# Two steps' attention scores issued together into the two halves of a PSUM bank

## What is computed

```python
h = rms_norm(x, g_mix);  proj = h @ w_in            # q, k, v of both kinds, two gates
ya = moba_attention(qa, ka, va, bias_a)             # 8 heads, causal
yb = swa_attention(qb, kb, vb, sinks, bias_b)       # 8 heads, window 128, a sink each
merged = sigmoid(ga + ...) * (ya @ w_branch_a) + sigmoid(gb + ...) * (yb @ w_branch_b)
x = x + merged @ w_out
x = x + square(relu(rms_norm(x) @ w_ff1)) @ w_ff2
```

## Time and profile before

| what | value |
|---|---|
| median of 3 runs | 724.69 us (723.51 to 725.76) |
| profiled execution | 726.15 us, its span 724.4 us |
| mean granted TensorE clock | 0.995 |
| PE busy | 709.8 us, 98% |
| PEld (weight loads) busy | 580.1 us, 80% |
| DVE, ACT, POOL busy | 382.3, 312.3, 331.8 us |
| attention stage (steps 0 to 31) | from 125.8 to about 277 us of the span |
| DMA | 96 GB/s in the mean |

### The profile page before, as it was taken

The page is one execution under the profiler, slowest core; times in us unless marked ns, Lnnn a source line. Parts: engine busy times, 40 slices in busy tenths (PEclk is TensorE's granted clock), DMA queues, the critical chain, the costliest instruction groups (busy, mean ns, idle before and its releaser), DMA issues.

```text
span 724.4 us, 9461 instructions
## 1 busy us (share of the span) xinstructions
PE 709.8 (98%) x3434; PEld 580.1 (80%) x3434; DVE 382.3 (53%) x551; ACT 312.3 (43%) x572; POOL 331.8 (46%) x207
## 2 busy tenths in 40 slices
PE   8898999999999999899999999999999999999998
PEld 6686888888888888787888888888888888888887
DVE  5786653455445453886875521255113551166787
ACT  7575773566656554553443411333212431233220
POOL 4464664455554444343344454344444344344442
PEclk9999999999999999999999999999999999999999
DMA  8221333222221211442322322322322322322231
GB/s 272 85 88 59 111 102 111 75 73 75 86 80 54 88 58 59 138 142 99 108 96 90 114 87 93 111 87 87 116 87 87 110 93 87 115 88 88 89 115 58
DMA packets 22910, 69.89 MB, mean 96 GB/s; under 512 B 2731, under 2 KB 4267, under 8 KB 22876
## 3 DMA queue, kind: packets, MB, share of 16 engines
q1 hardware_dynamic: 22876, 69.44, 29.1%
HBM read 67.27 MB, written 2.16 MB: 96 GB/s over the span
## 4 chain that ended last, share of the span: by engine, by line
PE 88%; DVE 7%; ACT 1%; DMA 1%; issue 1%; SPq 1%; DVEq 0%; ACTq 0%
PE bank L882 27%; PE bank L883 26%; PE bank L884 26%; PE bank L996 3%; PE bank L1007 2%; DVE probs L800 2%; PE bank L1024 2%; PE bank L1026 1%; DVE store L617 1%; DMA w_raw<-slabs 1%; DVE probs L790 1%; DVE x_lo L802 1%; DVE probs L788 1%; DVE store L621 1%; ACT x_hi L542 1%
## 5 line engine op out<-in xcount | busy, mean ns | idle before, releaser
L308 POOL TENSOR_TENSOR w_lo<-w_raw,w_hi 128x1024 fp32r<-128x1024 f32 x111 | 268.3, 2417 | 295.8 <-ACT w_hi L369 295.8
L882 PE MATMUL bank<-x_hi,w_hi 128*128 128x512 f32 (+1 forms) x600 | 237.5, 396 | 3.4 <-DVE x_lo L608 2.1
L883 PE MATMUL bank<-x_lo,w_hi 128*128 128x512 f32 (+1 forms) x600 | 232.6, 388 | 0.0
L884 PE MATMUL bank<-x_hi,w_lo 128*128 128x512 f32 (+1 forms) x600 | 232.5, 387 | 0.0
L369 ACT ACTIVATE w_hi<-w_raw 128x1024 fp32r<-128x1024 f32 x112 | 118.5, 1058 | 142.2 <-PE bank L884 142.2
L882 PEld LDWEIGHTS bank<-x_hi,w_hi 128*128 128x128 f32 x600 | 113.0, 188 | 34.9 <-issue 5.1
L884 PEld LDWEIGHTS bank<-x_hi,w_lo 128*128 128x128 f32 x600 | 113.0, 188 | 23.6
L883 PEld LDWEIGHTS bank<-x_lo,w_hi 128*128 128x128 f32 x600 | 113.1, 188 | 21.4
L882 PE MATMUL bank<-qk_hi,w_hi 128*128 128x512 f32 x320 | 125.9, 394 | 1.8 <-DVE w_lo L796 1.8
L884 PE MATMUL bank<-qk_hi,w_lo 128*128 128x512 f32 x320 | 125.3, 391 | 0.0
L883 PE MATMUL bank<-qk_lo,w_hi 128*128 128x512 f32 x320 | 125.1, 391 | 0.0
(11 more groups left out here) (103 smaller groups left out, 649.4 us busy)
## 6 DMA issues: line engine op xcount, KB each, us to landing
w_raw<-slabs SPq DMA_DIRECT2D x112, 512.0 KB, 3.3
store<-x_t SPq DMA_DIRECT2D x16, 256.0 KB, 2.8
bias_m<-tab_dram SPq DMA_DIRECT2D x8, 256.0 KB, 4.5
out<-store SPq DMA_DIRECT2D x7, 256.0 KB, 2.0
bias_m<-tab_dram SPq DMA_DIRECT2D x8, 128.0 KB, 3.8
w_raw<-slabs SPq DMA_DIRECT2D x2, 384.0 KB, 5.7
w_raw<-slabs SPq DMA_DIRECT2D x2, 128.0 KB, 4.4
out<-store SPq DMA_DIRECT2D x2, 128.0 KB, 1.7
```

The costliest lines, as they stand in the source:

```text
L308: pool.tensor_tensor(w_lo[:, g % WS, :], w_raw[:, g % RAW, :], w_hi[:, g % WS, :].bitcast(F32), ALU.subtract).then_inc(w_lo_ready, 1)
L882: pe.matmul(out_, wh, xh, start=first, stop=False)
L883: pe.matmul(out_, wh, xl, start=False, stop=False)
L884: last = pe.matmul(out_, wl, xh, start=False, stop=end)
```

## The change

Where two steps' scores fit one bank side by side, `scores` issues both steps' passes at the even step, the second step's into columns 256 and up of the same bank, and nothing at the odd one. This is so for steps 0 to 15 in pairs (256 and 256 columns, or 256 and 128) and for the last two steps of each causal pair (256 and 128 columns: steps 18 and 19, 22 and 23, 26 and 27, 30 and 31). The causal steps with 512 and 384 columns stay single. The wait for `max_ready` stays at every step that issues scores, and is gone from the 12 odd steps that issue none. `scores_max` of an even step of a pair waits for two units more, that is for the second step's scores in the same bank. Transposes, gate halves and values stay where they were; the number of matmuls is the same.

```diff
+        def scores_at(i, e, qt):
+            at = S // 2 if (qt % 2 == 0 if i < 8 else qt == 0) else 0
+            return bank[3 + e][:, at:at + P * key_tiles(i, qt)[1]]
+
+        def score_steps(step):
+            if STEPS // 2 <= step and step % QT < 2:
+                return (step,)
+            return (step, step + 1) if step % 2 == 0 else ()
...
             def scores_max(u, i, e, qt):
...
-                dve.wait_ge(scores_done, u + 1)
+                step = u // 2
+                dve.wait_ge(scores_done, u + 3 if len(score_steps(step)) == 2 else u + 1)
...
-                    out=probs[:, u % 4, 0:n], in0=bank[3 + e][:, 0:n], in1=bias_m[:, i % 4, 0:n],
+                    out=probs[:, u % 4, 0:n], in0=scores_at(i, e, qt), in1=bias_m[:, i % 4, 0:n],
...
             def scores(step):
-                if step:
+                steps = score_steps(step)
+                if step and steps:
                     pe.wait_ge(max_ready, 2 * step)
-                for a in range(3):
-                    for u, i, e, qt in units(step):
+                for of in steps:
+                    for a in range(3):
+                        for u, i, e, qt in units(of):
...
-                        last = pe.matmul(bank[3 + e][:, 0:P * nk], q, k, start=(a == 0), stop=(a == 2))
+                            last = pe.matmul(scores_at(i, e, qt), q, k, start=(a == 0), stop=(a == 2))
```

More of the change, by code:

```diff
@@ L987, in scores @@
             def scores(step):
-                if step:
+                steps = score_steps(step)
+                if step and steps:
                     pe.wait_ge(max_ready, 2 * step)
-                for a in range(3):
-                    for u, i, e, qt in units(step):
-                        k0, nk = key_tiles(i, qt)
-                        q = (qk_lo if a == 1 else qk_hi)[HEADS[e], q_tile(i), P * qt:P * qt + P]
-                        k = (qk_lo if a == 2 else qk_hi)[HEADS[e], k_tile(i), P * k0:P * (k0 + nk)]
-                        last = pe.matmul(bank[3 + e][:, 0:P * nk], q, k, start=(a == 0), stop=(a == 2))
-                        if a == 2:
-                            last.then_inc(scores_done, 1)
+                for of in steps:
+                    for a in range(3):
+                        for u, i, e, qt in units(of):
+                            k0, nk = key_tiles(i, qt)
+                            q = (qk_lo if a == 1 else qk_hi)[HEADS[e], q_tile(i), P * qt:P * qt + P]
+                            k = (qk_lo if a == 2 else qk_hi)[HEADS[e], k_tile(i), P * k0:P * (k0 + nk)]
+                            last = pe.matmul(scores_at(i, e, qt), q, k, start=(a == 0), stop=(a == 2))
+                            if a == 2:
+                                last.then_inc(scores_done, 1)
             def probs_transpose(step):
```

## The result

The changed kernel takes 718.72 us (median of 7, 717.36 to 722.05); the kernel before took 725.06 us in the same sessions (median of 7, 723.51 to 726.65). The ratio is 0.9913, with a 95% interval of 0.9893 to 0.9934. The profiled execution took 718.83 us, its span 717.0 us against 724.4.

A forecast was written before the change was run, and what follows sets the result against it. PE's own stream was taken to bound the attention stage. Merges giving 1.5, 1.4 and 2.4 us, together 5.3 us, came off the 724.69 us median, forecasting 719.4 us, range 717.4 to 722.1 us.

The forecast's parts named there:

- What bounds the stage: Attention stage: bound by PE's own stream, so time taken out of it comes off unless a wait replaces it.
- The hole is the array's change of mode, not the wait: Ahead of scores on PE: 0.17 us hole in all 32 steps, from changing 128-row columns to 64-row halves, not `max_ready`.
- The odd steps: Twelve odd steps lose their scores group: 0.68 us removed with 128 columns, 0.74 us with 256.
- The added passes: Even step's group on PE: three further passes add 0.36 us with 256 columns, 0.34 us with 128.
- dear seam: Rival: second step's passes start afresh, each merge pays 0.55 us; gain 2.8 us, 721.9 us; chance 0.10.
- DVE's wait: Even step's `scores_max` waits for both steps' scores: sliding chain moves 0.34 to 0.36 us, causal chain 0.08 us.
- The stall itself: PE's wait for `y_sums` before `values` at steps 18, 22, 26, 30: 0.40 us, falling to 0.14 us.
- The small waits inside `values`: PE's 0.15 us wait at steps 6, 10 and 14 neither grows nor goes.
- The sum: Twelve merges: 1.5 us and 1.4 us from sliding pairs, 2.4 us from causal ones, together 5.3 us.
- a case by itself: Clock rival: fall to 1.2 GHz behind the attention absent (717.8 us) or twice as long (721.0 us); chance 0.10.

The follow-up runs named there:

- the kernel before with `y_sums` first: Kernel before the change, with DVE's `y_sums` put ahead of `gate_scale` in steps 6, 10, ... 30; median 722.52 us, ratio 0.9966.
- the two kernels without it: Kernel before and changed kernel, each with DVE's `y_sums` ahead of `gate_scale`; medians 722.52 and 717.82 us, steps 18 and 19 together 10.80 and 10.45 us.
- the run with the waits: Changed kernel with the 12 waits for `max_ready` put back at the odd steps that issue no scores; median 719.92 us, ratio 0.9934.
- that with `y_sums` first: DVE's `y_sums` put ahead of `gate_scale`, nothing else; run on the changed kernel (717.82 us) and on the kernel before (722.52 us).
- the kernel with split groups: Changed kernel with the second step's scores moved behind the first three gate matmuls of the even step, without a wait; median 730.86 us, ratio 1.0103.
- the one with the sliding half alone: Changed kernel with pairs of steps for the sliding heads only, every causal step issuing its own scores; median 721.22 us, ratio 0.9963.

## Why the prediction was right

- **What bounds the stage.** PE's own stream: what was taken out of it came off the time, and nothing behind the attention gave it back (5.69 us at the end of the loop and at the end of the stall alike).
- **The hole is the array's change of mode, not the wait.** That it comes with the group is shown from both sides: 12 waits with no group cost 0.17 us in all, 12 groups with no wait 0.43 us each where nothing else waits. That within the group it is the change from 128 rows to two halves of 64, and the array running empty for it, is argued: from the loads that start only with their matmuls, and from the ends that grow with the matmul in front. The Trainium skill, TensorEngine Tiling (Array Packing), section Key Properties, says that changing the tiling mode drains TensorE. The runs agree with it for the halves of the rows.
- **The odd steps.** Forecast 0.68 and 0.74 us, and the rows 0.69 us from transposes to the second gate product as forecast. By whole steps the odd ones are 0.67 to 0.71 us shorter with 128 columns and 0.75 to 0.78 with 256.
- **The added passes.** Forecast 0.34 us for three of 128 columns, measured 0.29: the one behind the seam's first needed 0.06 us and not 0.11. The dear seam fell.
- **DVE's wait.** Its start 0.31 us behind the last pass held exactly. At the causal steps the chain moved by 0.04 us and not 0.08, as the passes cost 0.29 and not 0.34 us, and the hole ahead of `values` fell to 0.17 us at step 18 (0.18 forecast) and 0.21 at the other three. The causal merges were worth 0.65 us each (0.60 forecast). The stall itself was sized too large, at 0.40 us: that is the hole in the weight loads, while PE lost 0.30 to 0.32 us by it, as the kernel before with `y_sums` first shows. It did not spoil the sum, because that goes by DVE's chain, which sets the length of the step in both kernels. The small waits inside `values` at steps 6, 10 and 14 were to stay at 0.15 us and grew to 0.21: DVE's second `y_sums` moved by 0.29 us, and PE reached `values` only 0.24 us later, as its 12 gate products took 2.85 us and not 2.89. Why they did is open. That it is the stall that takes up the difference is shown by the two kernels without it, 0.35 us.
- **The sum.** Forecast 5.3 us. The attention gave 5.7 (5.30 in the stretch and 0.4 for the first merge, ahead of it): the forecast was 0.4 us short. Most of it is some 0.05 us at each of the eight merges with a 128-column step (on PE in the sliding ones, in DVE's chain in the causal ones), the rest 0.02 to 0.03 us at each of the others.
- **The rest of the median.** The medians stand 6.3 us apart in the first session, and 6.7 (725.04 and 718.34) in the one in which the changed kernel was run again. With a mean clock of 0.997 and more on both sides they stand 4.9 apart. So the difference of the medians can't be told from 5.7 more closely than by about 1 us either way; in the two profiles the clock's part is 1.6 us, and seen. That the measured 718.72 us lies so near the forecast 719.4 is partly luck: a fall of the clock more or less moves an execution by more than that distance. The prediction had this as a case by itself, and set it against one fall behind the stall only; falls also come and go at 8 and at 26 us.

## What to carry to other kernels

Where matmuls that use half the array's rows stand between full ones, count the groups and not the matmuls: here a group cost 0.4 us in its ends and 0.1 us for each further pass. Putting two groups together is worth that, as long as the reader of the shared bank has time to wait for both. Before pricing such a merge, look whether PE stands idle a little later in the same step: a longer group in front of an idle hole was nearly free (0.04 us), and a merge was worth 0.65 us there where it gave 0.35 without the hole. And size such a hole by the matmuls, or by a run without it: in the weight loads it looked larger (0.44 us) than what it cost (0.30 to 0.32).

## What the runs showed that was not expected

- A wait on a semaphore whose value is long there costs PE nothing that shows: 12 of them made 0.17 us, no more than the 0.23 us between two profiles of one kernel.
- The second pass of 128 columns starts 0.06 us behind the first where the three follow the seam, and 0.16 us behind it at the head of a group of its own; the third follows the second by 0.11 us in both the earlier trace rows.
- Matmuls on half of the array's columns stand among full ones without a hole, 0.17 us for a pair of the two kinds; those on half of its rows don't.
- The granted clock falls to the 1.2 GHz level in some executions and not in others of the same kernel, in three places: at 8 us, at 26 us and behind the stall near 290 us. A fall lasts for over 3 us, at 26 us in the run with the waits and at 8 us in that with `y_sums` first for over 6. In the profiles of the kernel with split groups and of the one with the sliding half alone none of them is there, in the others one or two. The stall of 1.83 us behind the attention was followed by a fall in some profiles and not in others, with the same work before it.
